# A trunk layer on one core: stores of queries, memory gates and gated outputs issued by ScalarE's queue instead of GpSimd's

## What is computed

```python
h = rms_norm(x, pre_norm[i])
proj = h @ w_in[m][j]
# proj is cut into three mixer parts, gate (1024 + 512) and memory queries (512)
b_gate, c_gate, u = jnp.split(p, 3, axis=-1)
z = c_gate * u                      # then a causal convolution of width 3 over tokens
mix = b_gate * conv(z)
mem_o = memory_cross_attention(mq, mem, mem_norm[i], w_mem_kv[i])   # 4 heads, 256 memory rows
y = (jnp.concatenate([mix, mem_o], axis=-1) * jax.nn.silu(gate)) @ w_out[i]
x = x + rms_norm(y, post_norm[i])
```

## Time and profile before

| what | value |
| --- | --- |
| time, median of 3 runs | 2220.6 us (2220.54 to 2221.02) |
| the profiled execution | 2222.47 us, its span 2220.6 us |
| granted TensorE clock of the core | 0.999 |
| PE busy in the span | 2191.1 us (99%) |
| DVE busy | 1218.6 us (55%) |
| ACT busy | 739.1 us (33%) |
| POOL busy | 100.8 us (5%) |
| queue of SP's transfers | 391.70 MB, 50.1% of 16 engines |
| queue of POOL's transfers | 75.53 MB, 10.4% of 16 engines |

### The profile page before, as it was taken

One profiled execution on the slowest core, in us unless ns is written; L12 is line 12 of the kernel. 1 busy time (PEld: TensorE's weight loads), 2 busy tenths in 40 slices (PEclk: granted clock), 3 DMA queues, 4 the chain that ended last, 5 costly groups with the idle time before them and its releaser, 6 DMA issues.

```text
span 2220.6 us, 27170 instructions
## 1 busy us (share of the span) xinstructions
PE 2191.1 (99%) x10106; PEld 1821.0 (82%) x10106; DVE 1218.6 (55%) x1933; ACT 739.1 (33%) x1332; POOL 100.8 (5%) x155
## 2 busy tenths in 40 slices
PE   9999999999999999999999999999999999999998
PEld 7888888788888887888888888888888788888886
DVE  7677867644244352444335328675754755555554
ACT  5343433411221331212113333535452533333332
POOL 0000000000000000000000000100000000000000
PEclk9999999999999999999999999999999999999999
DMA  3786677667666778856667665656667633334331
GB/s 140 276 308 234 256 276 258 239 232 249 205 209 217 263 263 314 305 190 208 209 209 258 226 215 195 221 199 220 198 206 296 220 125 110 119 133 133 129 123 63
DMA packets 144737, 468.95 MB, mean 211 GB/s; under 512 B 15808, under 2 KB 15840, under 8 KB 141280
## 3 DMA queue, kind: packets, MB, share of 16 engines
q1 hardware_dynamic: 123808, 391.70, 50.1%
q0 software_dynamic: 20800, 75.53, 10.4%
HBM read 330.85 MB, written 136.31 MB: 210 GB/s over the span
## 4 chain that ended last, share of the span: by engine, by line
PE 89%; DVE 5%; DMA 3%; issue 2%; ACT 1%; SPq 0%; POOL 0%; DVEq 0%; ACTq 0%; POOLq 0%
PE banks L1541 29%; PE banks L1543 29%; PE banks L1542 29%; DVE hop_lo L1146 2%; DMA slots<-w_split 1%; PE banks L1658 1%; DMA sums_kept<-raws 1%; PE banks L1714 1%; DVE x_in L1132 1%; DMA q_kept<-zb 0%; ACT probs L917 0%; PE banks L1562 0%; ACT hop_hi L849 0%; DVE rmax L1295 0%; PE banks L1547 0%
## 5 line engine op out<-in xcount | busy, mean ns | idle before, releaser
L1541 PE MATMUL banks<-hop_hi,slots 128*128 128x512 f32 x2632 | 1030.8, 392 | 10.3 <-DMA slots<-w_split 5.1
L1542 PE MATMUL banks<-hop_lo,slots 128*128 128x512 f32 x2632 | 1024.7, 389 | 0.0
L1543 PE MATMUL banks<-hop_hi,slots 128*128 128x512 f32 x2632 | 1024.6, 389 | 0.0
L1541 PEld LDWEIGHTS banks<-hop_hi,slots 128*128 128x128 f32 x2632 | 494.3, 188 | 117.2 <-issue 10.1
L1543 PEld LDWEIGHTS banks<-hop_hi,slots 128*128 128x128 f32 x2632 | 494.1, 188 | 103.3
L1542 PEld LDWEIGHTS banks<-hop_lo,slots 128*128 128x128 f32 x2632 | 494.4, 188 | 101.2 <-issue 1.4
L1174 DVE TENSOR_TENSOR slots<-raws,slots 128x512 fp32r<-128x512 f32 x156 | 106.8, 690 | 141.2 <-ACT slots L804 140.7
L860 ACT ACTIVATE s<-banks 128x512 f32<-128x512 f32 x94 | 56.3, 599 | 302.3 <-PE banks L1543 301.5
L1226 DVE TENSOR_TENSOR u<-banks,u 128x512 f32<-128x512 f32 x54 | 37.3, 690 | 213.9 <-PE banks L1543 213.9
L804 ACT ACTIVATE slots<-raws 128x512 fp32r<-128x512 f32 x156 | 96.8, 626 | 153.6 <-PE banks L1543 128.6
L804 ACT ACTIVATE slots<-st_w 128x512 fp32r<-128x512 f32 x144 | 90.2, 627 | 153.6 <-PE banks L1543 114.4
(11 more groups left out here) (169 smaller groups left out, 2085.4 us busy)
## 6 DMA issues: line engine op xcount, KB each, us to landing
slots<-w_split SPq DMA_DIRECT2D x406, 512.0 KB, 3.5
w_split<-slots SPq DMA_DIRECT2D x140, 512.0 KB, 3.0
raws<-in_w_in SPq DMA_DIRECT2D x86, 256.0 KB, 4.0
x_in<-in_x_t SPq DMA_DIRECT2D x16, 1024.0 KB, 7.2
g_kept<-mix POOLq DMA_DIRECT2D x32, 512.0 KB, 6.3
raws<-g_kept SPq DMA_DIRECT2D x64, 256.0 KB, 3.9
x_zb<-in_x POOLq DMA_DIRECT2D x22, 512.0 KB, 4.4
out_x<-x_zb POOLq DMA_DIRECT2D x21, 512.0 KB, 4.1
```

The source lines that it names most:

```text
L1541: nc.tensor.matmul(dst, a, c, start=first, stop=False, skip_group_check=True)
L1542: nc.tensor.matmul(dst, a, d, start=False, stop=False, skip_group_check=True)
L1543: return nc.tensor.matmul(dst, b, c, start=False, stop=last, skip_group_check=True)
```

## The change

`keep` moves from GpSimd's list to ScalarE's, with its waits and its transfers: 8 stores to q_kept, 8 to m_kept, 32 to g_kept. GpSimd keeps the 32 stores of attention heads (`keep_gated`), now one behind the other, and all of the output part. Where GpSimd issued the store of pair p - 1 as soon as its data were there, ScalarE issues it at a fixed place of its list: in step R5 of pair p, behind the copy of product R5 and ahead of `ahead` and `operand_hi`. Pairs 0 and 1 are stored behind the hi halves of R7 and R4 in the first pair's part, pair 79 in the second step of the output part.

```diff
-            for p in range((MACROS - 1) * PAIRS):
-                keep(p)
-            for step in range(PAIRS * PRODUCTS):
-                p, r = divmod(step, PRODUCTS)
-                if r == R5 and p:
-                    keep((MACROS - 1) * PAIRS + p - 1)
-                for n in range(HEADS):
-                    if step == WEIGH_AT[n] + 1:
-                        keep_gated(n)
-            keep(ALL_PAIRS - 1)
+            for n in range(HEADS):
+                keep_gated(n)
...
+            def keep(p):
+                m, i, kind = p // PAIRS, row_of(p), kind_of(p)
+                if kind == "q":
+                    act.wait_ge(c12_done, seven_to(p))
+                    act.wait_ge(c22_done, seven_to(p))
+                    act.wait_ge(c11_done, seven_to(p))
+                    act.wait_ge(copied, count("qcy", p) + 1)
+                    act.dma_start(kept_as(q_kept, m, i - FIRST_Q), zb[:, :, HALO:]).then_inc(q_kept_dma, 16)
+                if kind == "m":
+                    act.wait_ge(silu_done, silu_count(p, R4))
+                    act.dma_start(kept_as(m_kept, m, i), zb[:, :, HALO:] if p == 1 else mix[:]).then_inc(m_kept_dma, 16)
+                if kind == "g":
+                    group = (i - FIRST_C) // 4
+                    act.wait_ge(gated, 4 * (count("g", p) + 1))
+                    for f in range(2):
+                        act.dma_start(g_kept[2 * SUB * m:2 * SUB * (m + 1), group // 2, :, group % 2 * 2 + f, :].rearrange("s p n -> p s n"),
+                                       flat(mix[:, 2 * f:2 * f + 2, :]).rearrange("p (s n) -> p s n", n=P)).then_inc(g_kept_dma, 16)
...
             operand_hi(0, R7)
+            keep(0)
             first_outputs(6)
             first_outputs(7)
             operand_hi(0, R4)
+            keep(1)
...
                     evacuate(p, r)
+                    if r == R5 and p > DIRECT:
+                        keep(p - 1)
                     ahead(m, step)
...
                 if r in (R1, R5, R6):
                     evacuate(p, r)
+                if n == 1:
+                    keep(ALL_PAIRS - 1)
```

More of the change, by code:

```diff
@@ L712, in _ @@
                                pattern=[[-1, P]], channel_multiplier=1).then_inc(consts_set, 1)
[L714 to L733, removed]
             def keep_gated(n):
@@ L789, in square, with kept_as @@
                     nc.scalar.activation(sqt[:, k % 2, :], src, ACT.Square).then_inc(sq_done, 1)
+            def kept_as(kept, m, f):
+                return kept[m, 2 * f:2 * f + 2].rearrange("f t p n -> p (f t) n")
+            def keep(p):
[15 more added lines that the diff above has]
+                                       flat(mix[:, 2 * f:2 * f + 2, :]).rearrange("p (s n) -> p s n", n=P)).then_inc(g_kept_dma, 16)
             def root(tile, n=T):
```

## The result

The kernel after takes 2235.03 us (median of 4 executions, 2233.82 to 2236.07), the kernel before on the same chip 2220.81 (2220.54 to 2224.72): ratio 1.0059, 95% interval 1.0048 to 1.0071. That is 14.2 us more; forecast were 2.9. The profiled execution of after took 2234.77 us, its span is 2233.0, so 12.4 us more span than before (2220.6); the rest lies around the span and in the medians.

The account below looks back on a forecast made before the run. TensorE, busy 2191.1 of 2220.6 us, was taken to bound the kernel. Pair 61 1.3, passages 0.6, heads 0.3 and pair 80 0.7 summed to 2.9 us more: 2223.5 us, range 2219.8 to 2230.5.

Parts of the forecast that it names:

- rival 1: Long issues hold ScalarE's list in passages between macros; worst sum 11 us, 2231.6 us; chance 0.36, shared with a 10.9 us landing.
- Passages and heads: Issues ahead of hi halves in pairs 19, 39, 59, 0.2 us each; gated stores in 68, 72, 76, 0.1 each.
- Pair 39: The store lands before the sum at 797.95, so 0; with 7.7 us it would be 0.7 to 1.2 us late.
- Pair 61: Store of pair 60 lands later for VectorE's sum, with 7.7 us landing: +1.3 us, bounds -0.8 and +4.5.
- What is moved and costs nothing.: ScalarE's waits for gate stores in pairs 36, 37, 41, 63 are covered; DMA order and weights hardly change: 0.
- Rival 4: A store in a new place meets the weights' stream: one more 2.3 us wait, 2226 us; chance counted with the first rival.
- the sign that the prediction set for being wrong: TensorE waiting for weights in more than four places.
- Pair 80: Two issues behind VectorE's last gated product delay the weights ScalarE makes, then TensorE: +0.7 us, bounds 0 and +2.
- The chance of 0.36 for slower: Chance of ending over 0.2% slower, by long issues on ScalarE or by pair 61 alone with a 10.9 us landing.

Follow-up runs that it names:

- GpSimd's late version: The kernel before, with GpSimd's stores also waiting for ScalarE's copy of R5 of the next pair (pairs 0 and 1 excepted): 2227.27 us, ratio 1.0026.
- GpSimd with wide pieces: The kernel before, with queries and gates kept in runs of 8 KB a partition, issued by GpSimd: 2221.44 us, ratio 1.0002.
- The second one of after: The kernel after, unchanged, measured and profiled once more: median 2232.35 us, ratio 1.0055; the profiled execution took 2226.97 us.
- 8 KB pieces: The kernel after, with queries in a tile without halo columns and kept in DRAM in runs of 8 KB a partition: 2228.36 us, ratio 1.0032.
- 1 KB pieces: The kernel after, with queries kept in DRAM, and read back, in pieces of 1 KB: 2232.31 us, ratio 1.0046.
- the version with two tiles: The kernel after, with query and gate pairs written to two tiles in turn, so a pair waits for a store two pairs old: 2225.19 us, ratio 1.0017.
- queries back: The kernel after, with the 8 stores of queries back on GpSimd at their early place, gates and gated outputs staying on ScalarE: 2226.94 us, ratio 1.0023.
- ScalarE early: The kernel after, with stores of queries and gates issued behind the copy of R1 in place of R5: 2226.43 us, ratio 1.0021.

## Why the prediction was wrong

It named pairs 39, 61 and 80, but neither 63 nor 77 and 78. For both late landings it took a low value; its bounds held the wait of pair 61 (up to 4.5 us) but not that of pair 39 (1.2 at the most). And it lacked two mechanisms, the clock behind a stall and a store in front of a load.

- **"The issue takes long" (rival 1).** It fell as a mechanism: 0.37 us, with 0.1 exposed in a passage against 0.2 taken. The time of its worst sum, 2231.6, came nearer than the forecast's, for other reasons. No second issuing queue held ScalarE up: the eight issues of queries took 366 to 367 ns, six with an issue of SyncE running and two without. The Trainium skill, Perfetto Trace Analysis, section "DMA Instruction — HWDGE (DVE, Sync)", speaks of the sequencers of VectorE and SyncE; to carry it over to ScalarE was the prediction's own step, and these issues don't bear it out.
- **Passages and heads.** The issues exposed 0.05 us in pair 19 and 0.13 in pair 59 by the copies' starts, where 0.2 were taken, and nothing over 0.1 in pairs 68, 72 and 76, where 0.1 each were. With the 0.1 of pair 39 this is 0.3 us, where the forecast had 0.9.
- **Pair 39.** The failed step is "issued at 790.9 to 791.5 with 6.1 us, the median of the eight, it lands at 797.0 to 797.6 ... so 0". The 6.1 us were GpSimd's, and only GpSimd's at a place 4 us earlier (at the late place GpSimd's landed in 6.7). ScalarE's landed in 9.6; the wait of 2.65 us was priced at 0. The same sentence gave 0.7 to 1.2 us with 7.7. Pair 59, the twin, did hold: its store landed in 6.8 us without a wait.
- **Pair 61.** "I take 7.7, as this is a hardware queue beside other traffic" was the low choice: 9.2 us measured, 8.0 to 11.3 over the other profiles with these pieces. The upper bound, +4.5 with 10.9, had been argued away by a load that would have drained. But SyncE issued a load of key weights at 1217.48, which landed at 1224.13, and the next at 1225.64: the store of 1222.70 ran beside both. The wait grew by 2.56 us against 1.3 taken.
- **The clock is missing from the sum.** The prediction added waits only. Half clock behind the two stalls was 1.6 us on top of 2.65 and 3.0 on top of 2.56. The kernel that keeps TensorE busy shows it. Before, a wait of 2.32 us for weights had no such window behind it, so its trace alone didn't teach this.
- **"What is moved and costs nothing."** ScalarE did stand for the gate's store, and that was indeed covered: taking it away changed nothing. What failed is "The DMA engines carry the same bytes in the same order give or take 5 us; weights have four waits now ... I take 0". Before, the store of pair 62 had landed when the load of key weights in question was issued (1267.13 and 1267.84); after, issued 7.8 us later beside the loads, it leads that load by 0.35 us, and the load takes 8.5 us in place of 5.5. In GpSimd's late version the store follows the load by 0.53, and TensorE doesn't wait. In after this cost 2.3 us, and up to 4.1 where the clock fell behind it. Rival 4 had the price, 2.3, and was given no weight of its own. Weights are waited for seven times, the sign that the prediction set for being wrong; it is a weak one, as GpSimd with wide pieces, no slower than before, shows eight.
- **The gated stores** cost 1.2 us in waits for weights near pair 78 (0.19, 0.75 and 0.89 in place of 0.60), 1.8 us by the copies. The last one, 0.85 to 0.89 us (1.77 once), stands in every profile that has these stores on ScalarE's queue, and not with GpSimd issuing at the same place (one wait, 0.71 us). Why is open: the queue and the small packets changed together. The prediction had +0.3 for heads and 0 for this.
- **Pair 80** was right: +0.75 against 0.7, the wait 0.62.

Together: 2.65 + 1.6 in pair 39, 2.56 + 3.0 in pair 61 (0.3 less by the copies' starts), 2.3 in pair 63, 1.8 near 78, 0.75 in pair 80 and under 0.2 in the passages, less 2.0: 0.6 at the start, 0.6 in pairs 40 to 44 and 0.8 in pair 64. This is the account of one profile. The second one of after lost nothing in pair 39 and 1.1 us in pair 61, and 4.0 in pair 63, where the clock fell. The chance of 0.36 for slower leaned on the wrong mechanism, though its range of causes was the right worry.

What stays open: why a store in pair 39 lands in 6.9 or 9.5 us with one program, why 8 KB pieces help when 1 KB pieces don't hurt, and what makes the weights late near pair 78. On the load in pair 63 the Trainium skill, DMA: Bandwidth & Descriptors, section "Queues, rings and completion order", says that each DMA engine takes packets from its queues in turn. If the two then had equal shares, an estimate, the load would take up to twice its time: 8.4 to 9.0 us by the 4.2 to 4.5 of the block ahead of it, or 11 to 12 by the 5.5 to 6.1 that this block's own load took in the five profiles where no such store was in flight when it was issued. Measured were 8.1 to 8.8 in the eight profiles with the store issued 0.35 us in front on ScalarE's queue. That doesn't speak against the rule; that store and load really alternate was not seen.

## What to carry to other kernels

Moving a transfer to an idle engine's queue moves its place in time and gives it other landings. Here the place alone cost 5.5 us and the queue at that place 6 to 9 more, though the issue itself was cheap. Price it with the landing of that queue beside that traffic, take the longest row unless a run says otherwise, and look which load it now stands in front of. Where a tile's next writer waits for a store, use two tiles in turn before tuning the store; here a landing of 9.5 us then held up nobody. A stall of TensorE must be priced with the clock behind it: here 1.6 and 3.0 us on top of 2.65 and 2.56.

## What was unexpected of the hardware

- A DMA issue on ScalarE's queue took 0.37 us and overlapped the copy ahead of it (0.14 us after its start), so it exposed 0.1 us; GpSimd's took 0.75.
- The same stores make more packets on ScalarE's queue: 528 against GpSimd's 272 for 1024 KB in pieces of 2 KB, and 41728 against 8960 (20800 before less the 11840 that stayed) for all 33.56 MB, most of them for the gated outputs in pieces of 512 bytes.
- The clock at 0.50 came behind waits of 2.65 and 3.35 us, and behind one of 1.37 us in the version with GpSimd at the late place, behind the 2.34 us in pair 63 of the version with two tiles and behind 2.21 us there in after's second profile, but not behind 2.14 us in pair 61 of after's second profile or 2.06 in pair 63 of its first. This is GpSimd's late version, its windows:

```profile
1230.00:1232.00 2.00, 1.53 (x9) 1.36 (x10) 1.57 (x5) 0.26 (x1) 0.00 (x0) 1.00 1.00 387
1232.00:1234.00 2.00, 2.00 (x7) 1.57 (x6) 0.09 (x1) 0.00 (x0) 0.00 (x0) 0.55 0.26 107
```

- All these kernels have a wait of 2.04 to 2.18 us in pair 19. Behind it the clock fell in four of the sixteen profiles (GpSimd late, queries back, ScalarE early, two tiles), at 1.6 us each, of which 0.6 came back in pair 20, and not in the others. The windows of GpSimd's late version, then those of before:

```profile
417.00:419.00 2.00, 2.00 (x7) 1.51 (x6) 2.00 (x3) 0.26 (x1) 0.00 (x0) 0.50 0.00 0
```

```profile
417.00:419.00 2.00, 2.00 (x10) 1.65 (x9) 2.00 (x2) 1.50 (x1) 0.00 (x0) 1.00 0.04 14
```

The length of the wait alone doesn't tell whether the clock falls, and one profile against another can differ by 1.0 us behind a wait that no change touched.
